# A decoder layer on one core: pooling sums behind token-block sums, pooling maps inside the first stick-breaking steps

## The chip, the cores and the metric

The kernel runs on one core of one Trainium2 chip, in one launch. The metric is the device time of that launch in microseconds (us). A difference below 0.2% (4.0 us here) can hardly be told from no change with runs as scattered as these.

## What is computed

One layer works on x, 1024 tokens by 1024 channels, in float32. The part that matters here is the mixer between the first feed-forward block and the cross-attention:

```python
proj = h @ w_in                                     # h = rmsnorm(x); columns q | k | v | u, 512 each
# head group A: 8 heads x 64, stick-breaking attention, strictly causal
z = q @ k.T * scale
log_rest = where(strict, log_sigmoid(-z), 0)
suffix = cumsum(log_rest, reverse) - log_rest
a = where(strict, exp(log_sigmoid(z) + suffix), 0)
o_sb = a @ v
# head group B: 4 channel groups x 128, windows w = 2, 4, 8, 16
pooled[g] = (trailing sum of u[g] over w tokens) / count - u[g]
o_pool[g] = pooled[g] @ w_pool[g] * pool_scale
x = x + concat(o_sb, o_pool) @ w_out
```

Ahead of it stands `x += 0.5 * SwiGLU_1(rms(x))`; behind it come a cross-attention into 256 memory tokens, a second half-step SwiGLU and a final RMSNorm.

## The kernel before, in words

Every engine has its program written out by hand; semaphores join them. A matrix product in float32 is made of three passes: each operand is split into a high part (a ScalarE copy that rounds to the fp32r type) and a low part (VectorE: value minus high part, the helper `lo`, L2156), and TensorE adds low x high, high x low and high x high (`three`, L1113 to L1115) into a PSUM bank. So nearly every tile passes through ScalarE, then VectorE, then TensorE.

The mixer's projection goes in this order on TensorE. First the four channel groups of u, in two token halves each (units 0 to 7 of `a_units`; banks 4 to 7 in a ring). Then v, in four weight tiles: each tile adds to all eight banks, and the last one closes them (units 8 to 15). Then q and k together, by Strassen-like block products: seven products for each of NQ = 4 column blocks, in the order 1, 6, 7, 2, 5, 4, 3 (`q_multiply`, called "q products" below). The right-hand factors of products 6, 7, 5 are sums of four token-by-channel blocks, called T1, T3, T2, T4; I call them the token-block sums. For each c of 0 to 3 `q_right_sums(c)` makes four of them on VectorE and `q_right_lo` splits three of them; together they are the step ("right", c), a "right pass" below. The left-hand factors are sums of weight blocks, made on GpSimd (`q_left_sum`).

Pooling: GpSimd makes the trailing sums by doubling, one, two, three and four 128x1024 adds for g = 0 to 3 (L1033). After each g VectorE divides and subtracts the token, in place in `u_all`; that is the step ("mean", g), three instructions (L2610, L2612, L2615), and GpSimd begins g+1 only when ("mean", g) has signalled `s_pooled`. Then follow the pooling maps: one 128x128 map for each group and half (units A_PROJ to A_PROJ+7). For each, `pool_hi_part` and `pool_lo_part` split a piece of pooled u into one of four places, TensorE multiplies it (`pool_map`), ScalarE copies the result out, VectorE makes its low part, and that frees both the bank and the place.

The list `a_empty` holds what ScalarE and VectorE do behind the projection, in one fixed order: ("unit", k) empties a bank, ("split", n) splits weight tile n, ("right", c), ("last_right",), ("q_weight", p) and ("mean", g) are as above. TensorE may not begin v's tile n before split n (`a_lo`), nor add to a bank before the unit that held it is emptied (`a_free`). The copies of v's eight units (L2593) free the banks that the first q products use: product 1 of block 0 needs unit 12 copied, the fifth of the eight.

The q and k results are stored in DRAM (`q_store`), half by half, high and low part apart, and read back in another layout (`stack_load`), twelve 256 KB transfers for the first two heads, all from SyncE's queue. The semaphores `s_spill` count the stores that have landed.

Then the stick-breaking steps, s = 0, 1, 2, ...: TensorE makes the scores of one head and query block (`scores`), ScalarE takes two sigmoids of them (`rest`, L2021, and `beta`, L2037), VectorE scans `rest` (L2639, `stick`, one step later), GpSimd multiplies (L1094), four steps later TensorE transposes (`turn`, L1463) and nine steps later multiplies by v (`values`). The buffer `rest` lies where the q results wait for their store, so the sigmoid of step 0 waits for the last stores of half 0 and that of step 1 for those of half 1 (`act.wait_ge(s_spill[s], 64 * NQ)`). The first `turn` waits for all pooling maps to be emptied (`a_free, len(a_units)`).

## Time and profile before

| what | value |
|---|---|
| median of 3 runs | 2019.39 us (2018.32 to 2020.56) |
| the profiled execution, its own time | 2017.67 us |
| its span in the profile | 2015.9 us |
| TensorE busy | 1966.5 us, 98% of the span |
| VectorE, ScalarE, GpSimd busy | 69%, 44%, 31% |
| mean granted clock of TensorE | 0.995 of full |

The profiled execution is 1.7 us below the median; all places below are microseconds from its span's start. "Granted clock" is the share of full TensorE clock: 1.00 is 2.4 GHz and 0.5 is 1.2 GHz.

### The profile page before, as it was taken

How to read it: one execution, taken by the hardware profiler on the slowest of the kernel's cores; microseconds unless marked ns; L12 is line 12 of the kernel's file. 1: busy time of each engine (PE TensorE's matmuls, PEld its weight loads, DVE VectorE, ACT ScalarE, POOL GpSimd, SP SyncE). 2: the span in 40 equal slices, each digit the busy share in tenths (PEclk: the TensorE clock that was granted, in tenths of full speed). 3: DMA queues.
4: the chain of work that ended last, by engine and by line, in shares of the span. 5: the costliest groups of instructions: out<-in, count | busy, mean ns of one | idle time of the engine just before them, and what ended most of it. 6: DMA issues, size and time to landing. Idle time of an engine off the chain costs nothing.

```text
span 2015.9 us, 25288 instructions
## 1 busy us (share of the span) xinstructions
PE 1966.5 (98%) x9321; PEld 1619.6 (80%) x9321; DVE 1381.2 (69%) x1851; ACT 890.4 (44%) x1581; POOL 623.4 (31%) x456
## 2 busy tenths in 40 slices
PE   7999999999999989899999999999999999999998
PEld 6888888887887778766688888888888888878887
DVE  7765565559799786687655655568656556579897
ACT  6534434433445323587634443444433443434444
POOL 1354554530002244365321000221655455410001
PEclk9999999999999999999999999999999999999999
DMA  4223223245501112764234322240322322264102
GB/s 157 74 78 89 84 73 95 84 160 179 183 11 53 68 42 95 213 153 106 74 118 133 115 74 63 63 116 14 112 84 73 94 84 74 73 251 176 65 1 84
DMA packets 221251, 198.55 MB, mean 98 GB/s; under 512 B 7708, under 2 KB 172104, under 8 KB 221128
## 3 DMA queue, kind: packets, MB, share of 16 engines
q1 hardware_dynamic: 219952, 194.80, 31.1%
q10 hardware_dynamic: 1176, 2.12, 0.3%
q8 instruction: 75, 1.23, 0.3%
q14 instruction: 48, 0.39, 0.1%
HBM read 157.05 MB, written 39.85 MB: 98 GB/s over the span
## 4 chain that ended last, share of the span: by engine, by line
PE 59%; DVE 6%; ACT 2%; issue 1%; POOL 0%; DMA 0%; DVEq 0%; ACTq 0%; POOLq 0%
PE ps L1113 18%; PE ps L1115 18%; PE ps L1114 18%; PE ps L1482 1%; PE ps L1463 1%; DVE rest L2639 1%; DVE wb_lo L2156 1%; PE ps L1449 1%; DVE sr_lo L2156 1%; PE ps L1453 0%; ACT act_hi L1634 0%; DVE act_lo L2156 0%; ACT beta L2037 0%; ACT wb_hi L1634 0%; PE ps L1600 0%
## 5 line engine op out<-in xcount | busy, mean ns | idle before, releaser
L2156 DVE TENSOR_TENSOR w_lo<-st,w_hi 128x512 fp32r<-128x512 f32 x160 | 174.8, 1094 | 176.8 <-ACT w_hi L1634 176.7
L1113 PE MATMUL ps<-T_hi,w_lo 128*128 128x512 f32 x640 | 249.7, 390 | 0.5 <-issue 0.4
L1114 PE MATMUL ps<-T_lo,w_hi 128*128 128x512 f32 x640 | 249.3, 390 | 0.0
L1115 PE MATMUL ps<-T_hi,w_hi 128*128 128x512 f32 x640 | 249.3, 389 | 0.0
L1113 PE MATMUL ps<-tr_hi,sr_lo 128*128 128x512 f32 x616 | 242.2, 393 | 3.9 <-DVE tr_lo L2156 3.1
L1114 PE MATMUL ps<-tr_lo,sr_hi 128*128 128x512 f32 x616 | 240.1, 390 | 0.0
L1115 PE MATMUL ps<-tr_hi,sr_hi 128*128 128x512 f32 x616 | 240.0, 390 | 0.0
L1113 PE MATMUL ps<-B_hi,w_lo 128*128 128x512 f32 x576 | 226.4, 393 | 3.6 <-DVE B_lo L2156 2.8
L1114 PE MATMUL ps<-B_lo,w_hi 128*128 128x512 f32 x576 | 225.2, 391 | 0.0
L1115 PE MATMUL ps<-B_hi,w_hi 128*128 128x512 f32 x576 | 225.1, 391 | 0.0
L1113 PE MATMUL ps<-act_hi,wb_lo 128*128 128x512 f32 x384 | 152.7, 398 | 2.7 <-DVE wb_lo L2156 2.6
L1115 PE MATMUL ps<-act_hi,wb_hi 128*128 128x512 f32 x384 | 149.9, 390 | 0.0
L1114 PE MATMUL ps<-act_lo,wb_hi 128*128 128x512 f32 x384 | 149.8, 390 | 0.0
L1113 PEld LDWEIGHTS ps<-tr_hi,sr_lo 128*128 128x128 f32 x616 | 115.7, 188 | 33.1 <-DVE tr_lo L2156 9.0
L1113 PEld LDWEIGHTS ps<-T_hi,w_lo 128*128 128x128 f32 x640 | 120.2, 188 | 27.3 <-issue 2.8
L1115 PEld LDWEIGHTS ps<-T_hi,w_hi 128*128 128x128 f32 x640 | 120.2, 188 | 25.0
L1114 PEld LDWEIGHTS ps<-T_lo,w_hi 128*128 128x128 f32 x640 | 120.2, 188 | 24.7
L1634 ACT ACTIVATE sr_hi<-piece_A 128x512 fp32r<-128x512 f32 x110 | 69.5, 632 | 158.2 <-PE ps L1115 141.0
L1115 PEld LDWEIGHTS ps<-tr_hi,sr_hi 128*128 128x128 f32 x616 | 115.7, 188 | 24.3
L1114 PEld LDWEIGHTS ps<-tr_lo,sr_hi 128*128 128x128 f32 x616 | 115.7, 188 | 23.6 <-issue 0.2
L1634 ACT ACTIVATE w_hi<-st 128x512 fp32r<-128x512 f32 x160 | 99.9, 626 | 72.9 <-PE ps L1115 62.2
L1113 PEld LDWEIGHTS ps<-B_hi,w_lo 128*128 128x128 f32 x576 | 108.7, 189 | 28.1 <-issue 3.6
(321 smaller groups left out, 4331.2 us busy)
## 6 DMA issues: line engine op xcount, KB each, us to landing
gate_raw<-in_ffn_w_gate SPq DMA_DIRECT2D x44, 512.0 KB, 5.3
up_raw<-in_ffn_w_up SPq DMA_DIRECT2D x44, 512.0 KB, 5.1
h_spill<-up_s SPq DMA_DIRECT2D x66, 256.0 KB, 2.0
piece_A<-in_ffn_w_down SPq DMA_DIRECT2D x32, 512.0 KB, 4.4
piece_B<-h_spill SPq DMA_DIRECT2D x32, 512.0 KB, 6.3
wb_raw<-in_w_out SPq DMA_DIRECT2D x16, 512.0 KB, 3.7
wb_raw<-in_mem_w_kv SPq DMA_DIRECT2D x16, 512.0 KB, 3.8
wb_raw<-in_mem_w_q SPq DMA_DIRECT2D x16, 512.0 KB, 3.6
```

What stands on the lines that cost most here:

```text
L1113: pe.matmul(to, w_lo, m_hi, start=first, stop=False, skip_group_check=joins)
L1114: pe.matmul(to, w_hi, m_lo, start=False, stop=False, skip_group_check=joins)
L1115: return pe.matmul(to, w_hi, m_hi, start=False, stop=last, skip_group_check=joins)
L1449: pe.matmul(z, queries, k_lo2[slot][:, g, keys], start=True, stop=False)
L1463: mm = pe.transpose(ps[:, bank, (j - first) * P:(j - first + 1) * P], beta[m % BETAS][:, j * P:(j + 1) * P], ident[:])
L1482: mm = pe.matmul(o[:, lo:], v_all[:, j, hp * P + 64 * g:hp * P + 64 * (g + 1)], aT[:, AT_FIRST[b] + g * n + j, lo:], start=j == 0, stop=j ...
L1634: return act.activation(to, src, ACT.Copy, scale=scale)
L2156: return dve.tensor_tensor(to, value, plain(hi), ALU.subtract)
L2639: dve.tensor_tensor_scan(r[:, ::-1], r[:, ::-1], ps[:, STILL_BANK, 0:1].broadcast_to([P, n]), 1.0, ALU.mult, ALU.bypass).then_inc(s_scan, 1)
```

## The change

It moves work and removes none. On the chip's side the same matmuls, splits, sums and transfers are issued; two instructions are added, an early table load and a one-element sigmoid that brings it about, and the table load ahead of the first sigmoid goes.

```diff
--- before.py
+++ after.py
@@ -542,7 +542,7 @@
 
             return ap.bitcast(F32)
 
-        POOL_FIRST, POOL_AMONG = 4, ((0, 1), (1, 2), (2, 3), (3, 4))
+        POOL_FIRST, POOL_AMONG = 0, ((0, 2), (2, 4), (4, 6), (6, 8))
 
 
         wi = w_in[0]
@@ -559,7 +559,6 @@
                     a_empty.append(("split", n + 2))
                     a_done.append(len(a_units))
                 a_empty.append(("unit", len(a_units) - 1))
-        late = [("mean", 0), ("mean", 1)]
         u_done += a_done
         for n, (kind, j) in enumerate(A_TILES):
             if n < 2:
@@ -578,15 +577,12 @@
             a_done.append(len(a_units) if parts else None)
             if n + 2 < len(A_TILES):
                 a_empty.append(("split", n + 2))
-            a_empty += late
-            late = [("mean", j)] if kind == "u" else []
             if kind == "u":
                 u_done.append(len(a_units))
-            if n < 6:
-                a_empty.append(("right", n - 2))
-            elif n == 6:
-                a_empty += [("last_right",)] + [("q_weight", p) for p in (1, 6, 7)]
-        a_empty += [("q_weight", p) for p in (4, 3)]
+            a_empty += {2: [("right", 0)], 3: [("right", c) for c in range(1, QC)],
+                        4: [("mean", 0)], 5: [("mean", 1)],
+                        6: [("last_right",), *(("q_weight", p) for p in (1, 6, 7)), ("mean", 2)]}.get(n, [])
+        a_empty += [("q_weight", 4), ("q_weight", 3), ("mean", 3), ("pairs",)]
         A_PROJ = len(a_units)
         a_units += [("pool", g, half) for g in range(NG) for half in range(2)]
 
@@ -599,6 +595,8 @@
         for k, (kind, j, part) in enumerate(a_units):
             if kind == "v":
                 bank = (part + 4) % TC
+            elif kind == "pool":
+                bank = 5 + (k - A_PROJ - 1) % 3 if k > A_PROJ else 4
             else:
                 bank, ring = 4 + ring, (ring + 1) % 4
             a_after.append(holds.get(bank, 0))
@@ -685,7 +683,7 @@
             holds.update((b, m) for b in range(*z_bank[m]))
         assert all(end <= 4 for _, end in z_bank)
 
-        STILL_BANK = a_bank[A_PROJ + 4]
+        STILL_BANK = a_bank[A_PROJ]
         TURN_BANKS = [b for b in (4, 5, 6) if b != STILL_BANK]
         assert STILL_BANK != 7
 
@@ -836,20 +834,23 @@
             raw_load(0, 1)
             ffn_loads(0)
 
-            def stack_load(h):
-
-                if h in (0, 2):
-                    sp.wait_ge(p1_done, q_product(NQ - 1, 6 if h == 0 else 3))
-                    for slot in range(2):
-                        sp.wait_ge(s_spill[slot], 64 * (NQ - 1 if h == 0 else NQ))
-                elif h >= 4:
-                    sp.wait_ge(s_z, 2 * TC * (h // 2 - 1))
+            def stack_part(h, parts):
                 rows = slice(64 * h, 64 * (h + 1))
                 slot, g = (h // 2 + 1) % 2, h % 2
                 for to, lower, upper in ((q_stack, q_spill_hi, q_spill_lo), (k_hi2, k_spill_hi, k_spill_hi),
-                                         (k_lo2, k_spill_lo, k_spill_lo)):
+                                         (k_lo2, k_spill_lo, k_spill_lo))[parts]:
                     sp.dma_start(plain(to[slot][0:64, g]), lower[rows, :]).then_inc(s_stack[slot][g], 16)
                     sp.dma_start(plain(to[slot][64:P, g]), upper[rows, :]).then_inc(s_stack[slot][g], 16)
+
+            def stack_load(h):
+
+                if h == 2:
+                    sp.wait_ge(p1_done, q_product(NQ - 1, 3))
+                    for slot in range(2):
+                        sp.wait_ge(s_spill[slot], 64 * NQ)
+                elif h >= 4:
+                    sp.wait_ge(s_z, 2 * TC * (h // 2 - 1))
+                stack_part(h, slice(0, 3))
 
             def q_raw_load(i):
                 if i:
@@ -889,8 +890,14 @@
             q_raw_load(1)
             for i in range(NQ):
                 if i == NQ - 1:
-                    stack_load(0)
-                    stack_load(1)
+                    sp.wait_ge(p1_wlo, 7 * (q_mat(i) + 1))
+                    for slot in range(2):
+                        sp.wait_ge(s_spill[slot], 64 * (NQ - 1))
+                    for h in range(2):
+                        stack_part(h, slice(0, 1))
+                    sp.wait_ge(p1_done, q_product(NQ - 1, 6))
+                    for h in range(2):
+                        stack_part(h, slice(1, 3))
                 for k in ("c11", "c21"):
                     q_store(i, k)
                 if i + 2 < NQ:
@@ -1022,25 +1029,6 @@
             pool.wait_ge(s_pads, 4)
             pool.affine_select(out=neg, in_=plain(neg), compare_op=ALU.is_gt, fill=-2.0 ** 100, base=0,
                                pattern=[[-1, P]], channel_multiplier=1).then_inc(s_pads, 1)
-            links = 0
-            for g, w in enumerate(POOL_WINDOWS):
-                pool.wait_ge(a_free, u_done[g])
-                if g:
-                    pool.wait_ge(s_pooled, g)
-                src, step, k = u_all[:, g], 1, 0
-                while step < w:
-                    dst = (s0, s1)[k % 2]
-                    ins = pool.tensor_tensor(dst[:, PAD:], src[:, PAD:], src[:, PAD - step:PAD + SEQ - step],
-                                             ALU.add)
-                    step, src, k = 2 * step, dst, k + 1
-                    if step < w:
-                        links += 1
-                        ins.then_inc(s_pchain, 1)
-                        pool.wait_ge(s_pchain, links)
-                    else:
-                        ins.then_inc(s_wsum, 1)
-
-
             def q_left_sum(i, p):
                 if p == 5:
                     pool.wait_ge(q_in, 32 * (i + 1))
@@ -1075,8 +1063,29 @@
                     pool.wait_ge(p1_fold, q_fold(i, "t65"))
                     pool.tensor_tensor(made["s7"][:], q_s65[:], made["s7"][:], ALU.add).then_inc(p1_fold, 1)
 
-            for p in SUMS:
+            for p in (5, 6, 7):
                 q_left_sum(0, p)
+            pool.wait_ge(t_tlo, 16 + 12)
+            links = 0
+            for g, w in enumerate(POOL_WINDOWS):
+                pool.wait_ge(a_free, u_done[g])
+                if g:
+                    pool.wait_ge(s_pooled, g)
+                src, step, k = u_all[:, g], 1, 0
+                while step < w:
+                    dst = (s0, s1)[k % 2]
+                    ins = pool.tensor_tensor(dst[:, PAD:], src[:, PAD:], src[:, PAD - step:PAD + SEQ - step],
+                                             ALU.add)
+                    step, src, k = 2 * step, dst, k + 1
+                    if step < w:
+                        links += 1
+                        ins.then_inc(s_pchain, 1)
+                        pool.wait_ge(s_pchain, links)
+                    else:
+                        ins.then_inc(s_wsum, 1)
+
+
+            q_left_sum(0, 3)
             for i in range(NQ):
                 q_folding(i, "s16")
                 if i + 1 < NQ:
@@ -1951,6 +1960,7 @@
                 else:
                     for part in range(PLACES):
                         pool_hi_part(part)
+                    act.activation(fstat[:, 7, 1:2], ones[:, 0:1], ACT.Sigmoid)
                 q_out(i, "c21")
                 q_out(i, "c22")
                 if nxt:
@@ -1972,14 +1982,14 @@
                         q_right_hi("T4", c)
                 elif step[0] == "q_weight":
                     q_weight_hi(0, step[1])
+                elif step[0] == "pairs":
+                    for i in range(NQ):
+                        q_pair(i)
                 if step[0] != "unit":
                     return
                 k = step[1]
                 kind, j, part = a_units[k]
                 bank = ps[:, a_bank[k], :]
-                if k == A_PROJ:
-                    for i in range(NQ):
-                        q_pair(i)
                 if kind not in ("u", "v"):
                     act.wait_ge(a_out, k + 1)
                 if kind == "pool":
@@ -2577,13 +2587,13 @@
                         q_right_lo("T4", c)
                 elif step[0] == "q_weight":
                     q_weight_lo(0, step[1])
+                elif step[0] == "pairs":
+                    for i in range(NQ):
+                        q_pair(i)
                 elif step[0] == "unit":
                     k = step[1]
                     kind, j, part = a_units[k]
                     bank = ps[:, a_bank[k], :]
-                    if k == A_PROJ:
-                        for i in range(NQ):
-                            q_pair(i)
                     if kind == "u":
                         dve.wait_ge(a_out, k + 1)
                         dve.tensor_copy(u_all[:, j, PAD + part * HALF:PAD + (part + 1) * HALF], bank
```

In words: the four ("mean", g) steps and, on GpSimd, the trailing sums move behind the twelve splits of the token-block sums (`t_tlo` at 28); the first three weight sums of q block 0 move ahead of them, the fourth behind. No pooling map stands ahead of the steps any more; two stand in each of steps 0 to 3. Map 0 uses bank 4, which is not written again, the others share banks 5, 6 and 7. Of the first two heads' twelve loads the four of q go first, with a wait on the last weight split of q block 3 (`p1_wlo`) in place of the wait on its product 6 (`p1_done`); the wait on `s_spill` stays ahead of both. The following rows show three places.

On VectorE behind the copies of u's third group, before: the split of a weight tile, two mean steps, and the first instruction of the first right pass.

```order
L2156 TENSOR_TENSOR wa_lo<-wa_raw,wa_hi 128x1024
L2610 SCALAR_TENSOR_TENSOR u_all<-s,u_all 128x1022
L2612 TENSOR_TENSOR head_mean<-s,recip_count 128x2
L2615 TENSOR_TENSOR u_all<-head_mean,u_all 128x2
L2610 SCALAR_TENSOR_TENSOR u_all<-s,u_all 128x1020
L2612 TENSOR_TENSOR head_mean<-s,recip_count 128x4
L2615 TENSOR_TENSOR u_all<-head_mean,u_all 128x4
L2512 TENSOR_TENSOR q_tmp_T1a<-q_keep 128x512
```

The same place after the change:

```order
L2166 TENSOR_TENSOR wa_lo<-wa_raw,wa_hi 128x1024
L2522 TENSOR_TENSOR q_tmp_T1a<-q_keep 128x512
L2523 TENSOR_TENSOR q_tmp_T3a<-q_keep 128x512
L2525 TENSOR_TENSOR q_tmp_T2a<-q_keep,q_tmp_T1a 128x512
L2527 TENSOR_TENSOR q_tmp_T_0<-q_keep,q_tmp_T2a 128x512
L2166 TENSOR_TENSOR q_T_lo<-q_tmp_T2a,q_T_hi 128x512
L2166 TENSOR_TENSOR q_T_lo<-q_tmp_T1a,q_T_hi 128x512
L2166 TENSOR_TENSOR q_T_lo<-q_tmp_T3a,q_T_hi 128x512
```

Both mean steps are gone from here, and the right pass follows the split at once; the mean steps of groups 0 and 1 now stand behind the fourth right pass, each behind a split.

On VectorE ahead of the copies of v (`x_halves`), before: the last T4 split, the five weight splits of q block 0 and the copies.

```order
L2156 TENSOR_TENSOR act_lo<-q_tmp_T_3,act_hi 128x512
L2156 TENSOR_TENSOR q_w_lo<-q_raw,q_w_hi 128x512
L2156 TENSOR_TENSOR q_w_lo<-diag,q_w_hi 128x512
L2156 TENSOR_TENSOR q_w_lo<-q_raw,q_w_hi 128x512 x2
L2156 TENSOR_TENSOR q_w_lo<-q_st,q_w_hi 128x512
L2593 COPY x_halves<-ps 128x512 x8
```

After the change:

```order
L2166 TENSOR_TENSOR act_lo<-q_tmp_T_3,act_hi 128x512
L2166 TENSOR_TENSOR q_w_lo<-q_raw,q_w_hi 128x512
L2166 TENSOR_TENSOR q_w_lo<-diag,q_w_hi 128x512
L2166 TENSOR_TENSOR q_w_lo<-q_raw,q_w_hi 128x512
L2620 SCALAR_TENSOR_TENSOR u_all<-s,u_all 128x1016
L2622 TENSOR_TENSOR head_mean<-s,recip_count 128x8
L2625 TENSOR_TENSOR u_all<-head_mean,u_all 128x8
L2166 TENSOR_TENSOR q_w_lo<-q_raw,q_w_hi 128x512
L2166 TENSOR_TENSOR q_w_lo<-q_st,q_w_hi 128x512
L2603 COPY x_halves<-ps 128x512 x8
```

The mean step of group 2 now stands between the third and the fourth weight split, ahead of all eight copies.

On ScalarE at the start of the steps (`act_hi<-ps,gains` empties a map, `act_hi<-u_all` is a high part of a place, `q_hi_c` the high part of q and k results), before:

```order
L1634 ACTIVATE act_hi<-u_all 128x512
L1634 ACTIVATE act_hi<-ps,gains 128x512
L1634 ACTIVATE act_hi<-u_all 128x512
L2021 ACT_TABLE_LOAD
L2021 ACTIVATE rest<-ps 128x128
L2037 ACTIVATE beta<-ps 128x128
L1634 ACTIVATE act_hi<-ps,gains 128x512
L2021 ACTIVATE rest<-ps 128x256
```

After the change:

```order
L1643 ACTIVATE act_hi<-u_all 128x512 x4
L1963 ACT_TABLE_LOAD
L1963 ACTIVATE fstat<-ones 128x1
L1643 ACTIVATE q_hi_c<-q_s_1 128x512 x3
L2031 ACTIVATE rest<-ps 128x128
L2047 ACTIVATE beta<-ps 128x128
L1643 ACTIVATE act_hi<-ps,gains 128x512
L1643 ACTIVATE act_hi<-u_all 128x512
L1643 ACTIVATE act_hi<-ps,gains 128x512
L1643 ACTIVATE act_hi<-u_all 128x512
L2031 ACTIVATE rest<-ps 128x256
```

The table load stands ahead of the last three q_hi_c copies, and the sigmoids of step 0 ahead of the first emptied map; before, four maps were emptied ahead of them.

## Rows read from the trace of the kernel before

**Rows 1.** The page, busy time and share of the span of each engine.

```profile
PE 1966.5 (98%) x9321; PEld 1619.6 (80%) x9321; DVE 1381.2 (69%) x1851; ACT 890.4 (44%) x1581; POOL 623.4 (31%) x456
```

**Rows 2.** Timeline, TensorE: start, duration, line, tiles; in brackets idle time before.

```profile
713.25 0.39 PE L1113 MATMUL ps<-wa_hi,act_lo 128*128 128x512 f32 x1
...
722.69 0.80 PE L1113 MATMUL ps<-wa_hi,act_lo 128*128 128x512 f32 x1 [6.56 <-DVE u_all L2589]
...
765.92 0.39 PE L1113 MATMUL ps<-act_hi,q_w_lo 128*128 128x512 f32 x1
...
842.08 0.39 PE L1113 MATMUL ps<-act_hi,wp_lo 128*128 128x512 f32 x1
...
857.01 0.33 PE L1463 MATMUL ps<-ident,beta 128*128 128x128 f32 x1 [2.38 <-DVE act_lo L2598]
```

**Rows 3.** Busy time by stretch: PE, PEld, DVE, ACT, POOL; then TensorE clock, DMA.

```profile
716.00:730.00 14.00, 7.44 (x23) 5.85 (x23) 13.23 (x14) 2.62 (x4) 6.82 (x4) 0.76 0.30 85
857.00:872.00 15.00, 13.71 (x77) 10.65 (x77) 13.87 (x12) 13.07 (x25) 10.85 (x8) 0.89 1.04 274
```

**Rows 4.** Timeline, VectorE, from the first mean step on.

```profile
704.91 1.22 DVE L2610 SCALAR_TENSOR_TENSOR u_all<-s,u_all 128x1022 f32<-128x1022 f32 x1
...
712.46 2.38 DVE L2513 TENSOR_TENSOR q_tmp_T3a<-q_keep 128x512 f32<-128x512 f32 x1
...
743.04 0.69 DVE L2512 TENSOR_TENSOR q_tmp_T1a<-q_keep 128x512 f32<-128x512 f32 x1
...
748.35 1.23 DVE L2156 TENSOR_TENSOR wa_lo<-wa_raw,wa_hi 128x1024 fp32r<-128x1024 f32 x1
...
754.62 2.50 DVE L2156 TENSOR_TENSOR act_lo<-q_tmp_T,act_hi 128x512 fp32r<-128x512 f32 x4
...
760.04 3.07 DVE L2593 COPY x_halves<-ps 128x512 f32<-128x512 f32 x5
...
867.38 0.67 DVE L2656 COPY aT<-ps 128x512 f32<-128x512 f32 x1
```

**Rows 5.** Timeline, GpSimd, pooling sums, a weight sum and a later product.

```profile
706.54 1.89 POOL L1033 TENSOR_TENSOR s<-u_all 128x1024 f32<-128x1024 f32 x1 [12.70 <-DVE u_all L2615]
...
714.37 4.52 POOL L1033 TENSOR_TENSOR s<-s 128x1024 f32<-128x1024 f32 x2
...
735.49 1.73 POOL L1058 TENSOR_TENSOR q_st<-q_raw 128x512 f32<-128x512 f32 x1
...
866.76 2.82 POOL L1094 TENSOR_TENSOR beta<-beta,rest 128x1023 f32<-128x1023 f32 x2 [0.36 <-DVE rest L2639]
```

**Rows 6.** Timeline, ScalarE, q copies, first map, table load, sigmoids of steps 0, 4.

```profile
842.90 1.15 ACT L1634 ACTIVATE q_hi_c<-q_s 128x512 fp32r<-128x512 f32 x2 [3.38 <-DVE q_s L2533]
...
846.03 0.67 ACT L1634 ACTIVATE act_hi<-ps,gains 128x512 fp32r<-128x512 f32 x1
...
850.53 1.28 ACT L2021 ACT_TABLE_LOAD   x1
851.82 0.28 ACT L2021 ACTIVATE rest<-ps 128x128 f32<-128x128 f32 x1
...
856.22 0.92 ACT L2021 ACTIVATE rest<-ps 128x896 f32<-128x896 f32 x1 [0.21 <-POOL beta L1094]
```

**Rows 7.** Timeline, SyncE's queue, first stack load and two last stores: start, us.

```profile
831.36 0.51 SPq L851 DMA_DIRECT2D q_stack<-q_spill_hi  x1
...
844.64 0.43 SPq L867 DMA_DIRECT2D k_spill_lo<-q_s_r  x1
...
847.24 0.46 SPq L867 DMA_DIRECT2D q_spill_lo<-q_s_r  x1
```

**Rows 8.** DMA issues singly, those at 844.64 and 847.24: KB, us to landing.

```profile
k_spill_lo<-q_s_r SPq DMA_DIRECT2D x1, 256.0 KB, 5.2
...
q_spill_lo<-q_s_r SPq DMA_DIRECT2D x1, 256.0 KB, 5.1
```

## The prediction

> **What bounds the kernel now.** I read the page first: TensorE is busy for 1966.5 of 2015.9 us [rows 1], so a change that adds no matmul can win only where TensorE stands still or runs at the lower clock. Next I read TensorE's timeline through the mixer for idle time. Between the first u unit and the end of the q products there is one large hole: the second v block begins to wait at 716.13 and goes on at 722.69, 6.56 us, for a VectorE copy of u [rows 2]. The stretch around it has a granted clock of 0.76 against 1.00 [rows 3], and the first matmul behind the hole takes 0.80 us instead of 0.39 [rows 2]: TensorE came back at 1.2 GHz. The price: from 765.92 to 842.08 run 336 matmuls, 0.227 us each; from 722.69 to 765.92 run 180, which should take 40.8 us and took 43.2. So the hole costs 6.56 + 2.4 = 9.0 us. The q products then run without a hole to 842.08. Behind them come maps and first steps, with a 2.38 us wait at 857.01 for VectorE to empty the last map [rows 2], and again a lowered clock, 0.89 [rows 3].
>
> Why VectorE is late at the hole shows in its timeline: from 704.91 it does two mean steps, then the first right pass, and in it a 128x512 subtraction takes 2.38 us [rows 4] where the same one takes 0.69 at 743.04; GpSimd is in its 128x1024 adds then, which take 1.89 us alone and 2.26 each when VectorE works beside them [rows 5]. I read this as the two taking turns: one GpSimd add costs VectorE about 1.75 us, one VectorE subtraction costs 0.6.
>
> The Trainium skill ("SBUF — State Buffer", section "Who interferes with whom") has this as a lock: a VectorE instruction with two SBUF inputs and a GpSimd one that reads SBUF block each other for a whole instruction. It says as well that with at most one SBUF input, outside the two-port modes, VectorE does not contend. The trace agrees with both: the PSUM copy at 867.38 takes 0.67 us [rows 4] inside GpSimd's work from 866.76 to 869.58 [rows 5].
>
> **Part 1, the hole at the v blocks.** VectorE's work from 704.9 on, in its new order. A right pass alone takes 5.2 us (743.04 to 748.35, with the gap behind it) [rows 4].
> - First right pass to 710.1; copy of u3's first half (0.6) to 710.7. The second half is finished by TensorE only at 713.25 [rows 2], its copy ends 714.1. Bank 6, which the v block asks for at 716.13, is free by 710.7: the 9.0 us go.
> - The next weight split follows ScalarE's high part, about 1.0 us from 713.5, and takes 1.15 (the row at 748.35 has 1.23 with its tail [rows 4]): to 715.7.
> - Three right passes, 15.6. The three q weight sums on GpSimd now fall into them, since their load is issued behind that split; each costs VectorE 1.1 us, as a contended 512-wide one takes 1.73 [rows 5] and the turn of 0.6 lies in it. To 734.6.
> - Weight split to 735.75. TensorE is through two v blocks of 10.9 us (48 matmuls of 0.227) at 713.25 + 21.8 = 735.0 and waits for it: 0.9 us.
> - GpSimd starts pooling only now. Its g = 0 add 1.9, mean step 1.6 (704.91 to GpSimd's start at 706.54 [rows 4, 5]): 739.2. Weight split 740.4. Two adds of g = 1, 3.7: 744.1; mean 745.7.
> - Four T4 splits and three weight splits, 4.2 (four take 2.50 with the tail [rows 4]), in turns with the three adds of g = 2, 5.3: 755.2. Mean 756.8. Two weight splits and one add of g = 3: 759.8.
> - Five v copies, 3.07 [rows 4], which by the row at 867.38 take no turns: 762.8.
>
> TensorE has meanwhile done the last two v blocks, 735.9 + 21.8 = 757.7, and must wait for the fifth copy. So 5.1 us of the hole come back in front of the q products, since VectorE finishes that copy at 763.1 before and 762.8 after: it saves turns with GpSimd and loses as much waiting for sums that begin late. The q products start at 762.8 instead of 765.92, **3.1 us sooner**. What clock they start at no row shows. After 6.56 us idle 2.4 us were lost; after the q products the hole of 2.38 was followed by a lower clock too [rows 2, 3]. Nothing lost is one bound, 2.4 the other; I take the middle, 1.1. **Part 1: -2.0.** Bounds: if GpSimd's weight sums fall between VectorE's instructions and no T4 turn is lost, VectorE is ready before TensorE and q starts at 757.5 or so, -8.4; if it takes 1 us more and the clock costs 2.4, +0.3.
>
> Inside the q products nothing moves in: the weights of product 3 of block 0 are ready near 767 (last four adds of g = 3 to 764.5, weight sum 1.3, two splits), 11 us before its turn; the last mean step is done near 769. Both were hidden under TensorE and still are.
>
> **Part 2, the tail.** I count in the old times, as if the q products still ended at 842.08. The stack loads: the first is issued at 831.36 [rows 7], later than product 6 of block 3, which ends near 828.5 (three blocks of 19.04 and two products of 2.72 behind 765.92 [rows 2]). It was the landed stores that let it go, and that wait stays, so the swapped wait gains nothing: the loads are reordered, not earlier, 0. The scores of head 0 may wait a little for them; they stand ahead of the last stores in the same queue, so the store that the next paragraph waits for hides it.
>
> The sigmoid of step 0 waits for k's last stores of half 0: issued 844.64, landed 5.2 later, 849.8; step 1 for 847.24 + 5.1 = 852.3 [rows 7, 8]. Before, ScalarE filled that time with four maps and four places, 846.03 to 850.53, and then paid 1.28 for the table [rows 6]; step 0's sigmoid came at 851.82, so the stores cost nothing. Now the table load lies in the 3.38 us of idle time before 842.90 [rows 6] (saved: 1.28), but the maps stand behind the sigmoid, so ScalarE idles from 846.0 to 849.9. From there: two sigmoids 0.4, two maps and two places 2.2 (a pair takes 4.50 / 4 = 1.12, half of it the map [rows 6]): 852.5. Two sigmoids 0.5, again 2.2: 855.2. Step 2: 0.3 and two maps 1.1: 856.6. Step 3: 0.5 and two maps 1.1, with 0.2 to 0.5 of waiting for the last map, which needs bank 5 emptied by VectorE: 858.5. The first wide sigmoid, at 856.22 before [rows 6], starts near 858.6, and the first transpose, 857.01 before, near 859.4. **Part 2: +2.2.** Below, the narrower case is +1.0 (the lower clock that TensorE had at 857 falls away, ScalarE waits less); above, +4, if TensorE, idle for some 5 us before map 4, makes the last maps at 1.2 GHz.
>
> Sum: -2.0 + 2.2 = +0.2. On the profiled execution's 2017.67 that is 2017.9; on the median, 1.7 above it, 2019.6.
>
> By the skill's section again: it names copies among what can take both ports. If the v copies took turns with GpSimd's remaining adds, three turns of 1.75 would move the q start from 762.8 to 768.1, and the sum would be +5.5. The row at 867.38 is against it for PSUM sources.
>
> **The rivals.**
> - *VectorE is on time.* The turns cost less than I say. For it: VectorE has idle gaps in each right pass (0.7 us for ScalarE), where a GpSimd add may slip in. Against it: 2.38 at 712.46. Price: q starts at TensorE's own 757.5; -8.4 + 2.2 = -6.2, 2013.2. Half of it (q at 760.2, no clock loss, tail +1) gives -4.7, 2014.7.
> - *The tail pays off as well.* Only the table load counts, -1.3, because stores land sooner than the loads ahead of them let them now. For it: 5.2 and 5.1 us are long for 256 KB and come from the queue. Against it: the same twelve loads still stand ahead. -2.0 - 1.3 = -3.3, 2016.1.
> - *Slower: the maps go round one by one.* Seven maps share three banks, and each needs TensorE (0.7), ScalarE (0.6), VectorE (0.7) and three handovers (0.2 in all) before the bank is free: 2.2 us a round. I let rounds overlap. If those of maps 4 to 7 do not, they end at 852.7 + 8.8 = 861.5, and at 1.2 GHz a round is 2.9 and they end at 864.3; the first transpose comes near 865.8, tail +8.8, sum +6.8, 2026.2. It decides once the tail costs over 6.0. For it: the wait of 2.38 at 857.01 is just such a wait. Against it: with four banks before, 2.38 us was all that came of eight maps.
> - *The change does nothing*: neither hole was on the path. Excluded for part 1, where TensorE itself stands still.
>
> **Chances.** My forecast, two parts that cancel: 0.45, own range 2017.0 to 2022.5. VectorE on time: 0.25. Tail pays: 0.17. Slower: 0.13. The forecast's own case leaves little beyond 4.0 us to either side; VectorE on time gives most of "faster". So faster 0.28, within 0.2% 0.58, slower 0.14. The range of 8 in 10 reaches down into the first rival and up to half way to the slow one: 2013.0 to 2023.5.
>
> **What would show it.** Right: no hole at the second v block; a hole of 4 to 6 us right before the first q product, ended by a v copy; the q products' first matmuls partly at 0.5 clock; ScalarE idle 3 to 4 us before step 0's sigmoid, ended by a store; no table load behind the q products' last copies. Wrong: a hole under 2 us before the q products (first rival), the first transpose less than 15 us behind the end of the q products (14.9 before; I expect 17.3), or one over 21 us behind it. The prediction fails most easily on the length of VectorE's chain, since 1 us there is 1 us of TensorE.

## The result: 3.1 us slower, within what counts as no change

The median after the change is 2021.78 us (20 executions, 2020.26 to 2023.40), beside 2018.71 us for the kernel before on the same chip (20 executions). The ratio is 1.0015, 95% interval 1.0009 to 1.0022: 0.15% slower, surely not faster, and inside the 0.2% either way that the prediction calls the same, though the interval ends just beyond it. The ratios leave out two executions far above the rest, one here of the kernel before (2466.95 us) and one of e5 below (2813.32 us). 2019.6 was forecast, with a sum of +0.2; the sum is +3.1.

The page after; the line answers to [rows 1].

```profile
PE 1971.6 (98%) x9321; PEld 1620.2 (80%) x9321; DVE 1380.4 (68%) x1851; ACT 892.0 (44%) x1582; POOL 624.4 (31%) x456
```

TensorE runs the same 9321 matmuls in 5.1 us more. Where, its timeline after shows at the places of [rows 2]: first product of the v blocks, third v block, first q product, block 0's product 4, last q product, the fifth map, the first transpose of the stick-breaking (start, duration, line, tiles, idle time before).

```profile
715.51 0.39 PE L1122 MATMUL ps<-wa_hi,act_lo 128*128 128x512 f32 x1
...
739.56 0.50 PE L1122 MATMUL ps<-wa_hi,act_lo 128*128 128x512 f32 x1 [2.13 <-DVE wa_lo L2166]
...
764.05 0.47 PE L1122 MATMUL ps<-act_hi,q_w_lo 128*128 128x512 f32 x1 [0.79 <-DVE x_halves L2603]
...
781.94 0.47 PE L1122 MATMUL ps<-act_hi,q_w_lo 128*128 128x512 f32 x1 [1.27 <-ACT q_s L1643]
...
842.81 0.39 PE L1124 MATMUL ps<-act_hi,q_w_hi 128*128 128x512 f32 x1
...
854.49 0.80 PE L1122 MATMUL ps<-act_hi,wp_lo 128*128 128x512 f32 x1 [5.12 <-DVE act_lo L2608]
...
862.05 0.33 PE L1472 MATMUL ps<-ident,beta 128*128 128x128 f32 x1 [0.65 <-DVE act_lo L2608]
```

The hole of 6.56 us at the second v block is gone; new are waits of 2.13 ahead of the third v block, 1.27 inside the q products and 5.12 ahead of the fifth map. The stretches of lower clock have moved too (columns as in [rows 3]):

```profile
10.00:30.00 20.00, 15.11 (x57) 10.62 (x56) 16.58 (x34) 15.28 (x31) 0.00 (x0) 0.74 0.74 228
740.00:744.00 4.00, 4.00 (x12) 3.13 (x11) 2.00 (x4) 2.34 (x5) 2.87 (x2) 0.57 0.00 0
764.00:844.00 80.00, 77.28 (x336) 62.76 (x336) 46.32 (x53) 31.75 (x58) 39.72 (x27) 1.00 0.48 148
852.00:862.00 10.00, 6.91 (x20) 5.02 (x20) 9.17 (x16) 8.90 (x19) 1.46 (x3) 0.66 0.80 206
978.00:992.00 14.00, 12.25 (x81) 8.52 (x78) 8.26 (x9) 7.73 (x16) 5.04 (x4) 0.88 0.13 39
```

The first and the last of these stretches had, in the kernel before:

```profile
10.00:30.00 20.00, 15.11 (x61) 11.26 (x62) 16.75 (x36) 16.21 (x34) 0.00 (x0) 0.83 0.74 226
978.00:992.00 14.00, 12.25 (x80) 8.95 (x80) 6.92 (x8) 6.04 (x12) 2.19 (x2) 1.00 0.26 77
```

The spans (2021.2 and 2015.9) differ by 5.3 us. The first v product is already 2.26 us later (715.51 beside 713.25 [rows 2]), with the same code ahead of it and a clock of 0.74 instead of 0.83 at 10 to 30 us; the experiments below show 713.4 to 716.1 there whatever the edit. I leave that out and measure each stretch from the one before it:

| stretch, us | before | after | difference |
|---|---|---|---|
| first v product to first q product | 52.67 | 48.54 | -4.1 |
| first to last q product | 76.17 | 78.99 | +2.8 |
| end of q products to first transpose | 14.92 | 19.01 | +4.1 |
| first transpose to the last row of transposes of the stick-breaking | 127.21 | 127.98 | +0.8 |
| from there to the end | 1031.7 | 1031.2 | -0.5 |

(The q products are counted from the start of the first to 0.23 behind the start of the last.) The fourth line holds a gain of 0.8 right behind the first transpose, where the clock was lowered before ([rows 3], the stretch from 857) and is full after, and a loss of 1.1 near 986, where it is the other way round (0.88 and 1.00 above); its remaining 0.5 the fifth line gives back. Together +3.0, as the medians have it.

**The v blocks.** VectorE's timeline after, places as in [rows 4]:

```profile
707.17 0.69 DVE L2522 TENSOR_TENSOR q_tmp_T1a<-q_keep 128x512 f32<-128x512 f32 x1
...
736.55 2.96 DVE L2166 TENSOR_TENSOR wa_lo<-wa_raw,wa_hi 128x1024 fp32r<-128x1024 f32 x1
...
747.21 7.59 DVE L2166 TENSOR_TENSOR act_lo<-q_tmp_T,act_hi 128x512 fp32r<-128x512 f32 x4
...
758.52 2.39 DVE L2166 TENSOR_TENSOR q_w_lo<-q_st,q_w_hi 128x512 fp32r<-128x512 f32 x1
760.84 4.86 DVE L2603 COPY x_halves<-ps 128x512 f32<-128x512 f32 x8
```

And GpSimd's, places as in [rows 5]: g = 0's add, the last two adds of g = 2, the last three of g = 3, the fourth weight sum of q block 0, the first of block 1.

```profile
736.53 1.90 POOL L1077 TENSOR_TENSOR s<-u_all 128x1024 f32<-128x1024 f32 x1 [5.76 <-DVE q_T_lo L2166]
...
749.72 4.52 POOL L1077 TENSOR_TENSOR s<-s 128x1024 f32<-128x1024 f32 x2
...
760.44 6.66 POOL L1077 TENSOR_TENSOR s<-s 128x1024 f32<-128x1024 f32 x3
767.06 1.74 POOL L1052 TENSOR_TENSOR q_st<-q_raw,diag 128x512 f32<-128x512 f32 x1
...
776.41 1.29 POOL L1046 TENSOR_TENSOR q_st<-q_raw 128x512 f32<-128x512 f32 x1 [3.96 <-DMA q_raw<-in_w_in]
```

At 736.53 the add begins 0.02 us ahead of VectorE's weight split; the split takes 2.96 instead of 1.23 [rows 4], and that is 1.7 of TensorE's wait of 2.13.

**The q products.** The fourth weight sum is behind all the adds, at 767.06. What hangs on it is in ScalarE's and SyncE's timelines:

```profile
768.83 0.63 ACT L1643 ACTIVATE q_w_hi<-q_st 128x512 fp32r<-128x512 f32 x1 [4.84 <-POOL q_st L1052]
...
776.36 0.64 ACT L1643 ACTIVATE q_w_hi<-q_raw 128x512 fp32r<-128x512 f32 x1 [5.92 <-DMA q_raw<-in_w_in]
...
781.22 0.58 ACT L1643 ACTIVATE q_s<-ps 128x512 f32<-128x512 f32 x1
```

```profile
770.22 0.99 SPq L859 DMA_DIRECT2D q_raw<-in_w_in  x2
```

The load of block 1's raw weights may go only when block 0's last weight is split: 770.22, 6.17 us behind the first q product; before it was issued here, 2.25 behind:

```profile
768.17 0.99 SPq L858 DMA_DIRECT2D q_raw<-in_w_in  x2
```

ScalarE stands 5.92 us for it, the copies of products (`q_s`) queue behind, and TensorE waits 1.27 for the one of 781.22. At the same place of blocks 1 and 2 it waits again:

```profile
801.52 0.47 PE L1122 MATMUL ps<-act_hi,q_w_lo 128*128 128x512 f32 x1 [0.26 <-ACT q_s L1643]
...
821.15 0.47 PE L1122 MATMUL ps<-act_hi,q_w_lo 128*128 128x512 f32 x1 [0.34 <-ACT q_s L1643]
```

With the smaller gaps around these waits, block 0 takes 1.7 us more than before, blocks 1 and 2 take 0.5 and 0.6 more, and block 3 nothing: the 2.8.

**The tail.** ScalarE after, places as in [rows 6]: the table load, the sigmoid that makes it, step 0's and the first wide sigmoid.

```profile
840.49 1.28 ACT L1963 ACT_TABLE_LOAD   x1
841.79 0.20 ACT L1963 ACTIVATE fstat<-ones 128x1 f32<-128x1 f32 x1
...
851.37 0.28 ACT L2031 ACTIVATE rest<-ps 128x128 f32<-128x128 f32 x1 [4.29 <-DMA k_spill_lo<-q_s_r]
...
861.44 0.92 ACT L2031 ACTIVATE rest<-ps 128x896 f32<-128x896 f32 x1 [0.23 <-PE ps L1462]
```

SyncE's last stores that it waits for, as in [rows 7]:

```profile
845.60 0.43 SPq L868 DMA_DIRECT2D k_spill_lo<-q_s_r  x1
...
848.19 0.46 SPq L868 DMA_DIRECT2D q_spill_lo<-q_s_r  x1
```

The one of 845.60, singly, as in [rows 8]:

```profile
k_spill_lo<-q_s_r SPq DMA_DIRECT2D x1, 256.0 KB, 5.7
```

ScalarE idles 4.29 us with the maps queued behind, and TensorE 5.12 us, after which its first matmul takes 0.80: 1.2 GHz.

### The profile page after: what moved, and what is told of

Its sections match the earlier page's. It is cut to its first block, busy times and chain, and to the rows that moved or that the text cites. A ratio compares the mean times of both kernels' runs of the same rounds, so it can differ in the third digit from the quotient of the medians.

```text
span 2021.2 us, 25290 instructions
## 1 busy us (share of the span) xinstructions
PE 1971.6 (98%) x9321; PEld 1620.2 (80%) x9321; DVE 1380.4 (68%) x1851; ACT 892.0 (44%) x1582; POOL 624.4 (31%) x456
## 3 DMA queue, kind: packets, MB, share of 16 engines
q8 instruction: 75, 1.23, 0.3%
## 4 chain that ended last, share of the span: by engine, by line
PE 54%; DVE 7%; ACT 3%; issue 2%; POOL 2%; DMA 1%; SPq 0%; DVEq 0%; ACTq 0%; POOLq 0%
PE ps L1122 17%; PE ps L1124 16%; PE ps L1123 16%; PE ps L1491 1%; PE ps L1472 1%; DVE act_lo L2166 1%; DMA q_raw<-in_w_in 1%; POOL s L1077 1%; DVE q_w_lo L2166 1%; DVE rest L2649 1%; DVE wb_lo L2166 1%; PE ps L1458 1%; DVE sr_lo L2166 1%; PE ps L1462 0%; ACT beta L2047 0%
```

## The experiments

Each median is compared with the kernel before in the same job (2019.17, 2018.73 and 2018.58 us in the three jobs, the changed kernel against its own at +3.07); "v to q", "q" and "tail" are the first three stretches of the table above. The ratio is estimated by itself and can differ from that of the two medians by up to 0.0005.

**The parts one by one.** e1_sums_only keeps the four moved mean steps, sums and `("pairs",)` of the diff. e2_maps_only keeps the hunks on the maps, with `STILL_BANK` and `("pairs",)` to fit:

```diff
-        POOL_FIRST, POOL_AMONG = 4, ((0, 1), (1, 2), (2, 3), (3, 4))
+        POOL_FIRST, POOL_AMONG = 0, ((0, 2), (2, 4), (4, 6), (6, 8))
...
+            elif kind == "pool":
+                bank = 5 + (k - A_PROJ - 1) % 3 if k > A_PROJ else 4
```

e3_table_only adds only the early sigmoid on `fstat`; e4_stacks_only only the new order of the first twelve loads.

> Of the change only the new order of the pooling sums, mean steps and weight sums is kept; maps, table load and stack loads are as before. Theory, from the trace of the changed kernel: 4.1 us are won between the first v block and the first q product (52.67 us before, 48.54 after), and 2.8 lost inside the q products (76.2 before, 79.0 after), because the load of q block 1's weights is issued 2.1 us later in the program than before while TensorE is 1.9 us ahead, and ScalarE's copies queue behind it. Sum: -1.3 us. Rival: the 2.8 us come from the early table load or the moved maps; then this kernel gains 4.1 us.

> Of the change only the maps move into steps 0 to 3, with their new banks; the table load stays ahead of the first sigmoid. Theory: ScalarE now waits idle for the last stores (4.29 us in the changed kernel) with all eight maps still ahead of it, and here the table load of 1.28 us is hidden in that idle time as well if it is issued before the wait, or follows it if not. The first transpose comes 4 us later behind the q products, 3.3 of it last: +3.3 us, +4.6 if the table load follows the wait. Rival: the slower tail is due to the reordered stack loads or the early table load; then this kernel is within 1 us of before.

> Of the change only the early sigmoid that brings the table load ahead of the last q copies. In the trace of before the load takes 1.28 us at 850.53, and the stores that step 0's sigmoid waits for have landed at 849.8, so the sigmoid could start at 850.5 instead of 851.8; step 1's waits for 852.3 anyhow, where it started 852.7 before. Theory: -0.4 to -1.3 us. Rival: the stores, not the table, hold the steps, 0 us.

> Of the change only the reordered loads of the first two heads. Theory: in both kernels the loads are let go by the landed stores, 1.88 us behind TensorE's start of product 7 of block 3 or so in either; only the order changes, and head 0 is complete two transfers later, some 2.3 us, at 843.1 in the old times, ahead of the maps that stand before the scores here: 0 us. Rival: they do start sooner, and the stores behind them with them: up to -1 us.

| kernel | median | to before | ratio, 95% interval | v to q | q | tail |
|---|---|---|---|---|---|---|
| sums | 2019.19 | +0.0 | 0.9998, 0.9989 to 1.0007 | 48.49 | 79.04 | 15.31 |
| maps | 2023.67 | +4.5 | 1.0020, 1.0011 to 1.0029 | 52.82 | 76.16 | 20.44 |
| table | 2019.68 | +0.5 | 1.0002, 0.9993 to 1.0011 | 52.81 | 76.16 | 14.57 |
| stacks | 2019.01 | -0.2 | 1.0002, 0.9993 to 1.0011 | 52.70 | 76.17 | 14.93 |

The loss in the q products belongs to the sums and the loss of the tail to the maps: each comes alone as in the whole. The medians agree for the maps (+4.5, of +4.6 expected if the table load follows the wait). For the sums they show none of the 1.3 us expected (+0.0, with -2.2 to +1.4 us in the interval); the profile of e1 has them in its first two stretches (-4.2 and +2.9), beside 0.4 more in the tail and a stretch of lowered clock near 981 us. In the maps' kernel the table load itself waits for the store; the changed kernel, where it does not, has 1.4 us less tail (20.44 to 19.01), though the two differ in the sums and loads as well. Alone the early load gives 0.35:

```profile
850.67 1.28 ACT L2023 ACT_TABLE_LOAD   x1 [3.99 <-DMA k_spill_lo<-q_s_r]
```

Alone, the table load out of the way brings step 0's sigmoid forward by 1.4 us against the end of the q products, and step 1's then waits for the next store. So the rival of that run was nearly right: the stores leave 0.35 us of tail, and the median shows nothing:

```profile
852.79 0.29 ACT L2022 ACTIVATE rest<-ps 128x128 f32<-128x128 f32 x1
...
854.77 0.39 ACT L2022 ACTIVATE rest<-ps 128x256 f32<-128x256 f32 x1 [0.95 <-DMA q_spill_lo<-q_s_r]
```

**The fourth weight sum.** e5_sum3_first is the kernel with the sums alone and this; e7_after_sum3 is the changed kernel with this:

```diff
                 if g:
                     pool.wait_ge(s_pooled, g)
+                if g == 3:
+                    q_left_sum(0, 3)
                 src, step, k = u_all[:, g], 1, 0
...
-            q_left_sum(0, 3)
```

e8_sum3_table is e5 with the early table load, e11_sum3_table_stacks that with the loads' new order, so all of the change but the maps. The other edit, e6_after_maps_first, is the changed kernel with ScalarE's and VectorE's maps of steps 0 and 1 put ahead (ScalarE's part):

```diff
             for s in range(M + OUT_LAG):
+                if s < 2:
+                    for k in pool_among[s]:
+                        empty(("unit", k))
...
-                if s < len(pool_among):
+                if 2 <= s < len(pool_among):
```

e9_sum3_maps_first has both. e10_after_short_adds is the changed kernel with short adds; it leaves out nearly all of the trailing sums of g = 2 and 3:

```diff
-                    ins = pool.tensor_tensor(dst[:, PAD:], src[:, PAD:], src[:, PAD - step:PAD + SEQ - step],
+                    end = PAD + (SEQ if g < 2 else 16)
+                    ins = pool.tensor_tensor(dst[:, PAD:end], src[:, PAD:end], src[:, PAD - step:end - step],
```

> The kernel before with the pooling sums moved behind the token sums, as in the third part alone, but with the sum for weight 3 of block 0 put ahead of the last window's adds instead of behind them; maps, table load and stack loads as before. Theory (the last weight's split comes late, so block 1's raw weights are asked for late, and each of the four q blocks then waits): the q products take 76.2 us again instead of 79.0, the stretch from the first v product to the first q product stays near 48.5 (at most 0.9 longer, since the last window's adds end one sum later), the tail stays at 14.9 to 15.3, and the median is 2016 to 2016.7 beside a kernel before of 2019.2 (ratio 0.9985). Rival (it is the adds themselves, beside which the weight splits and copies run longer, that lengthen the q products): the q products stay near 79 and the median stays at that of the kernel before.

> The changed kernel, where ScalarE empties the four maps of stick-breaking steps 0 and 1 ahead of those steps' sigmoids (in the program it stood behind them), and VectorE those of step 1 ahead of the scan. Theory (the four us of the tail are ScalarE standing at the sigmoid of step 0, for the last k and q stores, with the maps queued behind it, so that the maps are not emptied in the time it idles): ScalarE empties in the idle time from 843.9, TensorE's 5.1 us wait ahead of the maps' product shrinks under 2 us, the tail goes from 19.0 back to 15 to 16, and the median falls 3 us under the changed kernel's, to about 2018.7, level with the kernel before. Rival (the maps' products and the banks they go round in, one after another at the lower clock, are the cost wherever they are emptied): the tail stays over 18 and the median within 1 us of the changed kernel's.

> The changed kernel whole, with the sum for weight 3 of block 0 ahead of the last window's adds. Theory: only the q products' 2.8 us come back (79.0 to 76.2), the tail keeps its 19.0, and the median is about 2019, 2.8 under the changed kernel. Rival as for the same edit alone: no change, 2021.8; a third way is that the earlier end of the q chain is lost in the tail's wait for the stores, but those move with the q products, so I expect no such loss.

> The kernel before with the pooling sums behind the token sums, the sum for weight 3 ahead of the last adds, and the table loaded early; maps and stack loads as before. Theory (the early table load alone is covered by ScalarE's wait for the stores, and gives 0 to 0.4 us): as without the table, 2016 to 2016.5, ratio 0.9985, the tail 14.6 to 15.0. Rival (with the q products 2.8 us sooner ended, the table load is bared): 1 us less again, 2015.3.

> The changed kernel with both repairs: the sum for weight 3 ahead of the last window's adds, and the maps of steps 0 and 1 emptied ahead of those steps' sigmoids. Theory (the two losses are separate, each repair alone gave 2.5 us in the median): they add, 5 us under the changed kernel, about 2016.7, q products 77.5 and tail near 17, so 1 to 1.5 us above the kernel with the maps where they stood before (2015.2). Rival (one repair takes the other's wait over): no better than either alone, 2019.3.

> The changed kernel, but GpSimd's adds of the last two windows (g = 2 and 3) run over 16 of the 1024 columns: it leaves out nearly all of those windows' sums, not an instruction, a wait or an order. Theory (VectorE's T4 splits take 7.6 us for four because they go in turns with the adds of g = 2, and weight 3's sum waits for those of g = 3): the four T4 splits take 2.5 to 2.8 us, TensorE's 0.8 us wait ahead of the q products is gone, the q products take 76.2 to 77.5 instead of 79.0, and the tail keeps its 19; the median is 3 to 3.5 us under the changed kernel, near 2018.5. Rival (the q loss is from the order and the loads, not from the adds' length): the q products stay at 79.

> All parts of the change but the maps, with the sum for weight 3 ahead of the last adds. Theory (the stack loads' new order changes nothing, as alone): as without it, 2015.1, ratio 0.998. Rival (with the stores ending sooner the first stack loads are now waited for): 0.5 to 1 us less, 2014.3.

| kernel | median | to before | ratio, 95% interval | v to q | q | tail |
|---|---|---|---|---|---|---|
| e5: sums, sum 3 first | 2016.09 | -2.6 | 0.9984, 0.9974 to 0.9993 | 47.57 | 76.95 | 15.25 |
| e7: changed, sum 3 first | 2019.33 | +0.6 | 1.0001, 0.9993 to 1.0010 | 46.77 | 77.84 | 19.26 |
| e6: changed, maps first | 2019.35 | +0.6 | 1.0002, 0.9993 to 1.0011 | 48.54 | 79.15 | 16.96 |
| e9: changed, both | 2016.57 | -2.0 | 0.9988, 0.9980 to 0.9997 | 47.50 | 76.63 | 16.38 |
| e10: changed, short adds | 2016.89 | -1.7 | 0.9987, 0.9979 to 0.9996 | 47.57 | 76.16 | 17.94 |
| e8: e5 and table | 2015.15 | -3.6 | 0.9979, 0.9971 to 0.9988 | 46.77 | 77.56 | 15.22 |
| e11: e8 and stacks | 2014.32 | -4.3 | 0.9981, 0.9972 to 0.9990 | 46.79 | 77.56 | 15.26 |

What decides about the q products is when block 1's load is issued. No run moves that load alone; this rests on ScalarE's wait for it in the traces and on the order of the kernels, in which the length of the q products follows the issue:

| kernels | load issued, us behind first q product | q products |
|---|---|---|
| e2, e3, e4, e10; before | 2.24; 2.25 | 76.16; 76.17 |
| e9, e5 | 4.30, 4.32 | 76.63, 76.95 |
| e7, e8, e11 | 5.03, 5.03, 5.04 | 77.84, 77.56, 77.56 |
| e6, after, e1 | 6.16, 6.17, 6.18 | 79.15, 78.99, 79.04 |

From 2.25 to 4.3 0.5 to 0.8 us are lost, from 5.0 to 6.2 about one for one. The loads have a cycle of their own, slower than TensorE's. In the kernel before those of blocks 1, 2 and 3 go out at 768.17, 788.36 and 807.94, so 20.2 and 19.6 us apart, while a block of products takes 19.04; they fall back from 2.25 to 3.40 and 3.94 us behind the start of the block of products then under way, and cost nothing yet. A first load that is late is therefore not caught up: in all eight kernels that issue it at 4.3 or later the q products end 72.3 to 73.0 us behind it, whenever they began, and in the five that issue it at 2.25 they end 73.9 behind it. With the sum in its new place (e5's GpSimd, VectorE and SyncE) the last split comes right behind the copies of v, at 764.85 instead of 769.50, though it now takes turns with the last adds:

```profile
759.27 1.29 POOL L1041 TENSOR_TENSOR q_st<-q_raw,diag 128x512 f32<-128x512 f32 x1 [5.14 <-DVE q_w_lo L2155]
```

```profile
764.85 2.38 DVE L2155 TENSOR_TENSOR q_w_lo<-q_st,q_w_hi 128x512 fp32r<-128x512 f32 x1
```

```profile
767.26 0.99 SPq L854 DMA_DIRECT2D q_raw<-in_w_in  x2
```

So the theory holds, but the load still goes out 2 to 3 us later against the start than before, and by that cycle the 76.2 that I expected in e5 and e7 were out of reach. From the first v product to the end of the q products it takes 124.5 us in e5, 124.6 in e7 and 124.3 in e8 and e11, beside 128.8 before and 127.5 after: 3 us, the amount expected. The kernels whose q products are 0.6 to 0.9 longer than e5's start them 0.8 sooner.

The short adds give the same from the other side: with all instructions in place and only their length gone, the four T4 splits take 2.54 us instead of 7.59, TensorE does not wait ahead of the q products, and these take 76.16. It refutes the order alone as the cause. Its median is 4.8 us under the changed kernel's against its own, more than the 3 to 3.5 expected: 1.0 ahead of the q products, 2.8 in them, and 1.1 in a tail that I expected to stay at 19; of these 0.7 are k's store, landed 7.5 us behind the q products instead of 8.3, for which I have no cause. The third v block keeps its wait of 2.14, since g = 0's add was left whole.

```profile
747.79 2.54 DVE L2167 TENSOR_TENSOR act_lo<-q_tmp_T,act_hi 128x512 fp32r<-128x512 f32 x4
```

The maps ahead of the sigmoids: ScalarE empties two maps and fills their places in the time that it stood idle, the wait for the store shrinks from 4.29 to 2.25, TensorE's from 5.12 to 2.62, and the tail by 2.05 (ScalarE, then TensorE, of e6):

```profile
846.46 0.67 ACT L1643 ACTIVATE act_hi<-ps,gains 128x512 fp32r<-128x512 f32 x1
...
847.55 0.68 ACT L1643 ACTIVATE act_hi<-ps,gains 128x512 fp32r<-128x512 f32 x1
...
851.00 0.28 ACT L2034 ACTIVATE rest<-ps 128x128 f32<-128x128 f32 x1 [2.25 <-DMA k_spill_lo<-q_s_r]
...
851.33 0.69 ACT L1643 ACTIVATE act_hi<-ps,gains 128x512 fp32r<-128x512 f32 x1
...
852.42 0.70 ACT L1643 ACTIVATE act_hi<-ps,gains 128x512 fp32r<-128x512 f32 x1
```

```profile
852.86 0.80 PE L1122 MATMUL ps<-act_hi,wp_lo 128*128 128x512 f32 x1 [2.62 <-DVE act_lo L2611]
```

The queue behind the waiting sigmoid is thus at least half of the tail's loss, and neither theory had the number right (15 to 16 expected by the one, over 18 by the other). But the edit does not do all that its expectation says: step 1's two maps stand ahead of step 1's sigmoid and still behind step 0's, which waits for the store, so they are emptied at 851.33 and 852.42, and the fifth map, at 1.2 GHz, comes behind them. The kernel before emptied four ahead of step 0's sigmoid. No run does that with the new banks, so whether the other 2.0 us against before's 14.92 are those two maps or the smaller number of banks stays open. Both repairs together give what they give apart (2.5 and 2.5, together 5.1 against the changed kernel).

e8 and e11 are the fastest kernels: 0.2% under before. Their medians are the numbers of the rivals (2015.3 and 2014.3), but their traces show the tail of e5, not one a microsecond shorter: step 1's sigmoid comes 11.0 us behind the q products in all three. So the further 0.9 and 0.7 us in the medians are within the intervals and not shown to come from the table or the loads.

## Why the prediction was right or wrong

- **The hole at the second v block goes, 9.0 us:** right; from 715.51 to 737.4 TensorE runs through two blocks.
- **VectorE's chain.** In old times (2.26 less): the weight sums and right passes done at 734.2 (734.6 forecast). The 0.9 us wait at the third v block is 2.13: I let the split go ahead of g = 0's add, and the add went first by 0.02 us. The T4 splits and weight splits took 9.3 us with g = 2's adds (9.5 forecast). The fifth v copy ended at 761.6 (762.8).
- **The wait ahead of the q products, 5.1 us, and the clock after it, 1.1:** wrong in place. TensorE came there at 761.0 and not 757.7: 1.2 lost by the longer wait, 1.7 because after it the clock was 1.2 GHz for most of four microseconds (0.57 in the row at 740: 0.43 times 4), and 0.4 in smaller gaps. It then waits 0.79 and starts at full clock. The start is 4.1 us sooner, 3.1 forecast, and no clock is lost behind it: by that step alone the part would have been -4.1. A hole under 2 us here was my sign for the first rival, VectorE on time. It misled: VectorE's fifth copy came 1.2 sooner than forecast, but the hole is short because TensorE came 3.3 later.
- **"Inside the q products nothing moves in ... Both were hidden under TensorE and still are": the step that failed, 2.8 us.** I had the end of the fourth sum's splits right (near 767 in old time, 767.9 in the trace) and asked only when product 3 needs that weight, 11 us later. I did not ask what else is released by its split: SyncE's load of block 1, which the code holds until block 0's weights are split, and behind it ScalarE's in-order queue. That load goes out 54.7 us behind the first v product after and 54.9 before: the q products started sooner, their next weights did not. And once late the loads stay late, since their cycle is longer than a block of products. -4.1 + 2.8 = -1.3 stand for part 1's -2.0, and so near only by luck: the start was 1.0 better and the clock 1.1 better than forecast, against 2.8 that were not forecast; with the sum moved up the load goes 51.9 behind (e5), and e5 and e7 keep 3 us more.
- **Stack loads reordered, not earlier, 0:** right (e4).
- **Part 2, +2.2:** right mechanism, mis-sized; +4.1 to the first transpose, its upper bound. The forecast's own places give +2.4 (859.4 beside 857.01), not +2.2. The wait for k's store ended 8.3 us behind the q products instead of 7.8 (issued 2.56 behind them as before, landing 5.7 instead of 5.2 us). From there to the first wide sigmoid 10.1 us instead of 8.7, of which 1.0 are ScalarE's waits for TensorE (0.62, 0.16 and 0.23): after its 5.12 us of idle time TensorE made the maps at 1.2 GHz, the case that I had put at the bound and not into the sum, although [rows 2, 3] show just that after the 6.56 us hole. Later 0.8 us come back.
- **The sum +0.2** missed +0.7 of part 1, +1.9 of part 2 less the 0.8, and 1.1 near 986. The last comes and goes with the kernel (e1, e3, e7, e8 and e9 have such a stretch, before, e2, e4, e5, e6, e10 and e11 not), and I have no cause for it.
- **The rivals.** VectorE on time: no, the turns cost what the rows said. The tail pays: no. Slower by rounds of maps: its price of +6.0 for the tail was not reached, and the waits ahead of the last maps are short.
- The Trainium skill ("SBUF — State Buffer", section "Who interferes with whom"): the lock is seen again (the splits of 2.39 and 2.96 us above, instead of 0.69 and 1.23). The eight v copies from PSUM take 4.86 us, 0.61 each, inside GpSimd's adds from 760.44 to 767.10: for them the section's sentence on at most one SBUF input holds, and its warning on copies, which I had priced at +5.5, does not.

## What to carry to other kernels

When an instruction is moved back on its engine, "ready before its turn" is asked of its consumer only; ask as well which loads wait for its buffer, since such a load, and the in-order queue behind it, can be the true deadline. If the loads' own cycle is longer than the work that uses them, a late first load is not caught up. Work put behind an instruction that waits for a DMA is work taken out of that wait: keep the filler ahead of it in the program. And a wait of several microseconds ahead of TensorE is priced with the matmuls that follow at 1.2 GHz, in the sum and not only at its bound.

## What the runs showed of the hardware beyond this

- GpSimd's add and VectorE's weight split begin 0.02 us apart in the changed kernel (736.53 and 736.55). The add, first, takes its 1.90 us; the split takes 2.96 instead of 1.23, so it stood for nearly all of the add.
- The wait ahead of the third v block lasts 2.06 to 2.16 us in all kernels with the moved sums. Behind it the clock fell in the changed kernel, e1, e5, e6, e9 and e10 and not in e7, e8 and e11, with the same work around it; the first row is e5's, the second e7's, both for 736 to 744. The fall makes 1.7 us in the changed kernel's profile, and I have no cause for its coming or not.

```profile
736.00:744.00 8.00, 5.84 (x19) 4.36 (x18) 5.80 (x6) 5.21 (x9) 4.88 (x3) 0.79 0.00 0
```

```profile
736.00:744.00 8.00, 5.93 (x27) 4.59 (x26) 5.22 (x5) 4.82 (x8) 5.29 (x3) 1.00 0.01 2
```

- The early table load costs its 1.28 us and no more: the sigmoid behind it starts 1.30 us after it (840.49 and 841.79).
